# Ten input slots of a mixer: six ahead of the attention, four between its heads

## The reference

```python
x = layer_norm(ALPHA * x + 0.5 * swiglu(x, ffn1...))
proj = x @ w_in[l]                              # 1024 -> 2560
u, gb, gc, h, q, k, v = jnp.split(proj, splits, axis=-1)   # 256,256,256,256,512,512,512
y_a = pool_mixer(u, pool_w[l], pool_scale[l])   # window means 2,4,8,16 minus u, then a product by groups
y_b = gated_conv_mixer(gb, gc, h, conv_w[l])    # gb * conv3(gc * h)
y_c = neighbourhood_attention(q, k, v, rpb[l])  # 8 heads of 64, bias and mask, softmax
y = jnp.concatenate([y_a, y_b, y_c], axis=-1) @ w_out[l]
x = layer_norm(ALPHA * x + y)
x = layer_norm(ALPHA * x + 0.5 * swiglu(x, ffn2...))
```

## Time and profile before

| | us |
|---|---|
| median of 3 runs | 2865.69 |
| the profiled execution | 2866.16 |
| its span in the trace | 2864.3 |
| ten slots, layer 1: from the first piece to the end of the last | 216.89 to 275.67 |
| pooling's product and attention, layer 1 | 275.67 to 303.66, 27.99 |
| the same, layer 2 | 790.72 to 818.88, 28.16 |

### The profile page before, as it was taken

The page is one execution under the profiler, slowest core; times in us unless marked ns, Lnnn a source line. Parts: engine busy times, 40 slices in busy tenths (PEclk is TensorE's granted clock), DMA queues, the critical chain, the costliest instruction groups (busy, mean ns, idle before and its releaser), DMA issues.

```text
span 2864.3 us, 51977 instructions
## 1 busy us (share of the span) xinstructions
PE 2746.6 (96%) x21608; PEld 2534.5 (88%) x21608; DVE 1593.2 (56%) x2293; ACT 1299.3 (45%) x1847; POOL 439.1 (15%) x183
## 2 busy tenths in 40 slices
PE   8999999999999999999899899999999999989998
PEld 7988799899969989988899798999998789978898
DVE  5557655755766565556632815555555753452555
ACT  4444544444454444456524455444445543445443
POOL 0000000000000000014125670000003313764000
PEclk9999999999999999999999999999999999999999
DMA  8765366576536646663314454665673332454563
GB/s 233 214 184 169 92 188 184 170 217 192 161 94 187 186 145 194 185 171 108 94 53 126 152 180 125 185 188 160 186 214 111 96 90 61 162 159 135 160 185 124
DMA packets 622972, 445.42 MB, mean 156 GB/s; under 512 B 28048, under 2 KB 589488, under 8 KB 622320
## 3 DMA queue, kind: packets, MB, share of 16 engines
q1 hardware_dynamic: 622832, 443.43, 52.3%
HBM read 442.32 MB, written 1.05 MB: 155 GB/s over the span
## 4 chain that ended last, share of the span: by engine, by line
PE 77%; DVE 9%; POOL 6%; issue 5%; ACT 3%; DMA 0%; SPq 0%; DVEq 0%; POOLq 0%; ACTq 0%
PE ps L388 17%; PE ps L390 16%; PE ps L389 16%; PE ps L404 6%; PE ps L405 6%; PE ps L406 6%; POOL w_lo L889 6%; PE ps L670 1%; PE ps L646 1%; DVE w_lo L889 1%; PE ps L1595 1%; PE ps L1585 1%; ACT w_hi L685 1%; DVE sq L947 1%; PE ps L1557 1%
## 5 line engine op out<-in xcount | busy, mean ns | idle before, releaser
L388 PE MATMUL ps<-in_hi,w_hi 128*128 128x256 f32 x4352 | 1250.1, 287 | 27.4 <-DVE in_lo L963 7.6
L685 ACT ACTIVATE w_hi<-raw 128x1024 fp32r<-128x1024 f32 x800 | 845.6, 1057 | 921.2 <-PE ps L390 603.6
L390 PE MATMUL ps<-in_hi,w_lo 128*128 128x256 f32 x4352 | 1236.1, 284 | 0.0
L389 PE MATMUL ps<-in_lo,w_hi 128*128 128x256 f32 x4352 | 1235.9, 284 | 0.0
L889 DVE TENSOR_TENSOR w_lo<-raw,w_hi 128x1024 fp32r<-128x1024 f32 x622 | 760.6, 1225 | 696.6 <-ACT w_hi L685 695.5
L388 PEld LDWEIGHTS ps<-in_hi,w_hi 128*128 128x128 f32 x4352 | 839.0, 193 | 50.5 <-issue 13.7
L389 PEld LDWEIGHTS ps<-in_lo,w_hi 128*128 128x128 f32 x4352 | 839.2, 193 | 7.2 <-issue 0.5
L390 PEld LDWEIGHTS ps<-in_hi,w_lo 128*128 128x128 f32 x4352 | 838.8, 193 | 0.0
L889 POOL TENSOR_TENSOR w_lo<-raw,w_hi 128x1024 fp32r<-128x1024 f32 x178 | 438.5, 2470 | 2179.5 <-ACT w_hi L685 2178.6
L404 PE MATMUL ps<-w_hi,hid_hi 128*128 128x512 f32 x704 | 276.4, 393 | 1.2 <-DVE ps L1058 1.2
L405 PE MATMUL ps<-w_lo,hid_hi 128*128 128x512 f32 x704 | 276.0, 392 | 0.0
(11 more groups left out here) (327 smaller groups left out, 2636.5 us busy)
## 6 DMA issues: line engine op xcount, KB each, us to landing
raw<-in_w_ffn_in SPq DMA_DIRECT2D x176, 512.0 KB, 3.7
raw<-in_w_mix SPq DMA_DIRECT2D x112, 512.0 KB, 3.7
raw<-in_ffn_w_gate SPq DMA_DIRECT2D x88, 512.0 KB, 3.8
raw<-in_ffn_w_up SPq DMA_DIRECT2D x88, 512.0 KB, 3.7
raw<-in_ffn_w_down SPq DMA_DIRECT2D x88, 512.0 KB, 3.6
raw<-in_w_ffn_out SPq DMA_DIRECT2D x88, 512.0 KB, 3.6
raw<-in_w_in SPq DMA_DIRECT2D x40, 512.0 KB, 3.7
raw<-in_w_out SPq DMA_DIRECT2D x32, 512.0 KB, 4.2
```

The costliest lines, as they stand in the source:

```text
L388: nc.tensor.matmul(o, lh, rh, start=first, stop=False, **kw)
L389: nc.tensor.matmul(o, lh, rl, start=False, stop=False, **kw)
L390: return nc.tensor.matmul(o, ll, rh, start=False, stop=last, **kw)
L685: nc.scalar.activation(w_hi[:, e % SPLIT, :], raw[:, e % RAW, :], ACT.Copy).then_inc(sem("split_high"), 1)
```

## The change: what it does

The slots are loaded and multiplied in the order q, q, k, k, v, v, pool, gate c, h, gate b (`SLOTS1_ORDER`). The first six are multiplied ahead of the attention, as before. The eight pieces of the other four are multiplied by `fill` in the iterations i = 0 to 7 of TensorE's attention loop, one in each, and the pooling's product in i = 8. ScalarE's splits for them, and the copies of the four slots, go into `take`, at the end of its iterations. VectorE's low parts for the pieces three further on go into `beside(i)`, i = 0 to 7, at the end of its iterations; behind them there stand the pooling's sums (i = 2) and means (i = 3), the convolution's first two steps (i = 6), its other taps (i = 7) and its last product (i = 8). The bias masks move ahead, between the low parts of the six slots. The splits of the mixers' result move to i = 8 and later.

```diff
+SLOTS1, HEAD_SLOTS = 10, 6
+SLOTS1_ORDER = (4, 5, 6, 7, 8, 9, 0, 2, 3, 1)
...
 # TensorE
-                pe_linear(pe, 0, E1_IN, [features] * 8 + [tokens] * 2, C1_IN, TOGETHER)
+                pe_linear(pe, 0, E1_IN, [features] * 4 + [tokens] * 2, C1_IN, TOGETHER)
...
+                def fill(pieces):
+
+                    i = next(filled)
+                    if i < 2 * (SLOTS1 - HEAD_SLOTS):
+                        q, c = HEAD_SLOTS + i // 2, i % 2
+                        e = E1_IN + 2 * HEAD_SLOTS + i
+                        if c == 0 and q >= HEAD_SLOTS + 2:
+
+                            pe.wait_ge(sem("linear_taken"), q - 1)
+                        pe.wait_ge(sem("split_low"), e + 1)
+                        for _, o, left, right, first, last in features(2 + q % 2, e - c)[c]:
+                            mm = three(o, left, right, first, last, skip_group_check=True)
+                        mm.then_inc(sem("piece_used"), 1)
+                    elif i == 2 * (SLOTS1 - HEAD_SLOTS):
...
-                pe_attention(pe, "att", NA_HEADS, scores, values)
+                pe_attention(pe, "att", NA_HEADS, scores, values, fill)
...
 # ScalarE
+                def take(pieces):
+
+                    i = next(taken)
+                    if i < 2 * len(others):
+                        act_split(act, E1_IN + 2 * HEAD_SLOTS + i + SPLIT)
+                        if i % 2:
+                            nc.scalar.activation(others[i // 2], two_tiles(2 + (HEAD_SLOTS + i // 2) % 2), ACT.Copy)\
+                                .then_inc(sem("linear_taken"), 1)
+                    elif i == 2 * len(others):
+                        act.wait_ge(sem("pool_ready"), 1)
...
-                act_attention(act, "att", NA_HEADS, outs, beside=beside)
-                act_in_split(act, C1_OUT, mix1, mixed, first=2)
+                act_attention(act, "att", NA_HEADS, outs, take, beside)
+                act_in_split(act, C1_OUT, mix1, mixed, first=3)
...
 # VectorE
                 def beside(i):
-                    if i == 1:
-                        low_part(dve, E1_OUT + 2)
-                    if i in (3, 4):
-                        dve_in_split(dve, C1_OUT, mix1, first=i - 3, end=i - 2)
-
-                dve_double_bias(dve, steps, 1)
+                    if i < NA_HEADS:
+                        low_part(dve, E1_IN + 2 * HEAD_SLOTS + 3 + i)
+                    if i == 2:
+                        pool_sums()
+                    if i == 3:
+                        pool_means()
+                    if i == 6:
+                        dve.wait_ge(sem("linear_taken"), HEAD_SLOTS + 3)
+                        steps.link(nc.vector.tensor_tensor(conv_z[:, :, 1:S + 1], gate_c[:, :, :], conv_h[:, :, :], ALU.mult))
+                        conv_taps(1)
+                    if i == 7:
+                        conv_taps(0, 2)
+                    if i == 8:
+                        dve.wait_ge(sem("linear_taken"), SLOTS1)
...
                 dve_attention(dve, steps, "att", NA_HEADS, 64 ** -0.5,
                               lambda h, t: na_bias[:, h, (2 - 2 * t) * GRID:(6 - 2 * t) * GRID], beside)
-                dve_in_split(dve, C1_OUT, mix1, first=2)
+                dve_in_split(dve, C1_OUT, mix1)
...
 # SyncE
-                sp_linear(sp, E1_IN, columns(w_in[l], 10, (8, 9)))
+                sp_linear(sp, E1_IN, columns(w_in[l], SLOTS1, (8, 9), SLOTS1_ORDER))
```

More of the change, by code:

```diff
@@ L11 @@
+import itertools
 from contextlib import ExitStack
@@ L1784, in _ @@
                 pe_ln_turn(pe, 1)
-                pe_linear(pe, 0, E1_IN, [features] * 8 + [tokens] * 2, C1_IN, TOGETHER)
+                pe_linear(pe, 0, E1_IN, [features] * 4 + [tokens] * 2, C1_IN, TOGETHER)
                 pe.wait_ge(const_here, 32)
[L1789 to L1794, removed]
+                filled = itertools.count()
+                def fill(pieces):
[10 more added lines that the diff above has]
+                    elif i == 2 * (SLOTS1 - HEAD_SLOTS):
+                        pe.wait_ge(sem("linear_taken"), SLOTS1 - 1)
+                        pe.wait_ge(sem("pooled"), 1)
+                        pe.wait_ge(sem("pool_w_here"), 64)
+                        for c in range(2):
+                            mm = nc.tensor.matmul(ps[:, 2, c * S:(c + 1) * S], pool_w[:, c, :], pooled[:, c, :],
+                                                  start=True, stop=True)
+                        mm.then_inc(sem("pool_ready"), 1)
                 def scores(h, t):
                     o = 64 * (h % 2)
-                    pe.wait_ge(sem("linear_taken"), min(9 + h, 10))
+                    pe.wait_ge(sem("linear_taken"), min(HEAD_SLOTS - 1 + h, HEAD_SLOTS))
                     return [(na_q[o:o + 64, h // 2, t * P:(t + 1) * P], na_k[o:o + 64, h // 2, :])]
@@ L1891, in _ @@
                 act.wait_ge(sem("pool_pads"), 1)
-                dests = [pool_in[:, :, POOL_PAD:POOL_PAD + S], gate_b[:, :, :], gate_c[:, :, :], conv_h[:, :, :],
-                         na_q[:, 0:2, :], na_q[:, 2:4, :], na_k[:, 0:2, :], na_k[:, 2:4, :],
-                         na_v[:, :, 0:S], na_v[:, :, S:2 * S]]
+                dests = [na_q[:, 0:2, :], na_q[:, 2:4, :], na_k[:, 0:2, :], na_k[:, 2:4, :], na_v[:, :, 0:S], na_v[:, :, S:2 * S]]
                 act_linear(act, 0, E1_IN, dests)
[L1896 to L1900, removed]
+                others = [pool_in[:, :, POOL_PAD:POOL_PAD + S], gate_c[:, :, :], conv_h[:, :, :], gate_b[:, :, :]]
+                taken = itertools.count()
+                def take(pieces):
[7 more added lines that the diff above has]
+                        act.wait_ge(sem("pool_ready"), 1)
+                        for c in range(2):
+                            nc.scalar.activation(mix1[:, c, :], ps[:, 2, c * S:(c + 1) * S], ACT.Copy,
+                                                 scale=vec1[:, V1["pool_scale"] + c:V1["pool_scale"] + c + 1])\
+                                .then_inc(sem("pool_out"), 1)
                 def outs(h):
@@ L2091, in _ @@
[L2091 to L2115, removed]
@@ new lines, in _, with pool_sums @@
+                dve_double_bias(dve, steps, 1)
+                lows(E1_IN + 10, E1_IN + 2 * HEAD_SLOTS + 3)
+                def pool_sums():
+                    n = S + 2 * POOL_PAD
+                    dve.wait_ge(sem("linear_taken"), HEAD_SLOTS + 1)
+                    steps.link(nc.vector.tensor_tensor(sum2[:, :, 0:n - 1], pool_in[:, :, 0:n - 1], pool_in[:, :, 1:n], ALU.add))
+                    steps.link(nc.vector.tensor_tensor(sum4[:, :, 0:n - 3], sum2[:, :, 0:n - 3], sum2[:, :, 2:n - 1], ALU.add))
+                    steps.link(nc.vector.tensor_tensor(sum8[:, :, 0:n - 7], sum4[:, 1:2, 0:n - 7], sum4[:, 1:2, 4:n - 3], ALU.add))
+                    steps.link(nc.vector.tensor_tensor(sum16[:, :, 0:n - 15], sum8[:, :, 0:n - 15], sum8[:, :, 8:n - 7], ALU.add))
@@ new lines, in pool_means @@
+                def pool_means():
+                    cnt = cst("pool_cnt", 2 * S).rearrange("p (c t) -> p c t", c=2)
+                    for g, (w, sums) in enumerate(zip(POOL_W, (sum2[:, 0], sum4[:, 0], sum8[:, 0], sum16[:, 0]))):
+                        o = 64 * (g % 2)
+                        lo = POOL_PAD - w // 2
+                        ins = nc.vector.tensor_tensor(pooled[o:o + 64, g // 2, :], sums[o:o + 64, lo:lo + S],
+                                                      cnt[o:o + 64, g // 2, :], ALU.mult)
+                    steps.link(ins)
+                    nc.vector.tensor_tensor(pooled[:, :, :], pooled[:, :, :], pool_in[:, :, POOL_PAD:POOL_PAD + S],
+                                            ALU.subtract).then_inc(sem("pooled"), 1)
@@ new lines, in conv_taps @@
+                def conv_taps(*taps):
+                    for tap in taps:
+                        for c in range(2):
+                            w = vec1[:, V1["conv_w"] + 2 * tap + c:V1["conv_w"] + 2 * tap + c + 1]
+                            z = conv_z[:, c, tap:tap + S]
+                            if tap == 1:
+                                ins = nc.vector.tensor_scalar(conv_y[:, c, :], z, w, None, ALU.mult)
+                            else:
+                                ins = nc.vector.scalar_tensor_tensor(conv_y[:, c, :], z, w, conv_y[:, c, :], ALU.mult, ALU.add)
+                        steps.link(ins)
@@ L2271, in d_rows, with columns @@
                 return d[:, c // P:c // P + 1, :] if isinstance(c, int) else d[:, bass.ds(c // P, 1), :]
-            def columns(w, n, token_slots=()):
-                for i in range(n):
+            def columns(w, n, token_slots=(), order=None):
+                for i in order or range(n):
                     c = i * S
```

19 lines of the change are left out of this document (6 added, 13 removed).

## The result

The changed kernel took 2876.5 us (median of 7, 2871.09 to 2880.8), the kernel before 2868.61 us in the same comparison (median of 7). The ratio is 1.0025, 95% interval 1.0013 to 1.0036: slower by 3.7 to 10.3 us. In a second comparison of the same pair it was 1.0031 (1.0019 to 1.0044). 2881 us was forecast, 2868 to 2889 as the range. The medians are 7.9 us apart, where the forecast's sum had 15.7.

What follows compares the result with a forecast made beforehand. TensorE, busy 96%, was taken to bound the kernel, but a ScalarE-VectorE loop to pace the changed attention: 2866.16 + 11.5 (loop) + 4.2 (clock) = 2881.9 us profiled, median 0.5 lower, stated as 2881; range 2868 to 2889.

Steps and rivals of the forecast that it cites:

- The loop: Attention: ScalarE's split, VectorE's low part, next bias, maximum and exponentials form a 5.60 us turn, against TensorE's 5.54 per iteration.
- walk: Step-by-step sum along the loop from T to the output product: 56.87 us, against 51.03 before.
- T: End of the sixth slot (the twelfth piece), where the walk starts; 252.63 in the kernel before.
- additions: VectorE's pooling sums, means and convolution steps behind the low part, 6.17 us inside the loop, plus taps, 1.82.
- The clock: Half clock after the stalls of heads 6 and 7: 2.1 us per layer, 4.2 in all.
- such a fall would cost nothing: Clock loss after an earlier attention stall, as head 6's, lies in the next stall; only that after head 7's counts.
- The stalls: TensorE idles about 2 us ahead of head 3's transposes and about 4 us each ahead of heads 6 and 7.
- The sum: Whole kernel: 2866.16 + 11.5 + 4.2 = 2881.9 us for the profiled execution.
- A: Rival: busy sums decide, all TensorE idling in the two attentions goes, -5.8 and -5.9 us, 2854; chance 0.08.
- B: Rival: loop holds but pooling and convolution find gaps, 48.9 us per layer, -2.2 each, 2861; chance 0.07.
- C: Rival: head 3's stall also loses clock and the first split shows, another 2.5 + 1.3 us per layer, 2889; chance 0.11.
- the first split: Split of the mixers' result, expected to end before TensorE's product needs it; otherwise about 0.6 + 0.7 us per layer.

Runs made afterwards that it cites:

- the warm matmuls: Changed kernel plus 3, 7 and 7 idle TensorE matmuls ahead of its waits for the probabilities of heads 3, 6 and 7; ratio 1.0016 to the kernel before.
- the kernel with the loop opened: Changed kernel with each VectorE low part one iteration later, behind the next head's maximum; ratio 0.9948 to the kernel before.
- the kernel with the additions moved: Changed kernel with pooling and convolution ahead of the low part in VectorE's `beside(i)`; ratio 0.9983 to the kernel before.
- the changed kernel again: Changed kernel run and profiled a second time, no edit; ratio 1.0031 to the kernel before.

## Why the prediction was right

- **The loop.** The prediction's walk gave 54.52 us from T to the last transposes; the profiles show 54.51 and 54.47. Its terms held one by one, as the splits above show. That the additions are inside it is shown by two experiments, one taking them out (7.2 us less; 8.0 by the walk, and nearly all of the rest is the 0.6 us by which the sums and means outlast the waits into which they were put) and one adding to them (2.9 us more, 2.9 expected). That the loop closes through the low part ahead of the next bias is shown by the one that opens it there, which ends at 46.8 us.
- **The clock.** I took 2.1 us per layer, 4.2 in all, within 0 to 2.5. Against the warm matmuls it cost 1.25 us in each layer of the first profile, 2.5 in all, and 2.0 and 2.5 in the second, 4.5 in all. So the term was 1.7 us too large for the execution that it was meant for and about right for the next one; which of the two a run gets was not foreseen, and that 2.1 met the second is luck as much as reading. The mechanism was right, for the loss counts behind the last stall. Expecting it of the stalls of about 4 us alone was not: the stall of 1.74 us at head 3 was followed by half clock in one profile (0.50 from 282.7 to 289.5) and by full clock in the other. That such a fall would cost nothing was right: nothing later moved.
- **The stalls.** Forecast were about 2, 4 and 4 us, some 10 per attention. Measured were 1.74, 1.26 and 3.95 in one profile, 7.0 in all, and 1.74, 3.98 and 3.08 in the other, 8.8. The half clock makes the difference: where TensorE works more slowly ahead of a wait, the wait is shorter.
- **The sum.** +15.7 us was forecast for the profiled execution, and it was +13.0 (2879.17 against 2866.16). At the output product of layer 2 it stood at 832.32 - 818.88 = 13.4; the two stages gave 58.12 - 51.03 and 58.11 - 51.20, 14.0 together, less some 0.6 gained ahead of them. As timed the change costs much less, 7.9 us by the medians and 7.2 by the ratio. Of the 13.0 us about 5 are the luck of the two executions that were profiled: the one before lies 2.5 us under the median of its seven runs, the one after 2.7 us over its own. The direction and the place of the loss were forecast rightly, its size as timed twice too large.
- **The rivals.** A, the busy sums, is refuted for this kernel, with a remark: its time is near that of the kernel with the loop opened, 46.8 us a layer against the 45.3 of A. The Trainium skill's advice to interleave regimes (Perfetto Trace Analysis, Optimization Strategy) holds in this case's runs once the order allows it (ratios 0.9983 and 0.9948 for the same work in other places of the lists), and not before (1.0025). B, additions that find gaps, describes the kernel with the additions moved (50.5 us per layer, 48.9 by B's sum), not the changed one. C did not happen: the stall of head 3 did lower the clock in the first profile, but the loss vanished in the later waits, and the first split did not show.
- **What stays open.** As timed the change costs 3.7 to 12.6 us by the two intervals, its two stages 14 and 15.4 in the two pairs of profiles (from T past the output product). All kernels built on the change come out 4 to 7 us better than their stages, by the ratios; the kernel against itself does not (1.0004). Behind the output product of layer 2, in parts that no kernel here changes, the profiles took from 2040.0 to 2046.7 us, and both of the kernel before lie high, at 2045.4 and 2045.6. One lead is the clock: over a whole run it was granted at 0.981 in the mean of 46 timed runs of the kernel before, and at 0.9815 to 0.986 in the means of the kernels built on the change, and among those 46 the longest runs have the low clock (2875 to 2877 us at 0.976 to 0.979, 2858 us at 0.982 and 0.983). Whether that is luck or a link to the changed part was not tested.

## What to carry to other kernels

When two engines hand work to each other inside one iteration, add up one turn start to start, with every instruction that stands between a wait and the next hand-over, and compare that sum with the bound engine's iteration, before believing busy shares. If the turn is as long as the iteration, there is no free place in it: put other work ahead of the wait, where the engine idles anyway, or take the waiting instruction one iteration later, so that it finds its input there. A stall that is removed can come back one instruction further down another engine's list, so read that list too. And measure a stage up to a point well behind it: what a stall costs through the clock can fall into the next one.

## What the runs showed of the hardware that was not expected

The granted clock does not fall at the same places from one execution to the next, with the same instructions in the same order. Besides 282 to 291 above, a stretch in the second layer of the second block shows it. Both kernels do the same work here, 120 us behind the first transposes of a norm. Before:

```profile
2274.70:2284.70 10.00, 4.32 (x30) 4.11 (x30) 9.47 (x22) 1.75 (x2) 0.00 (x0) 0.82 0.03 8
2284.70:2294.70 10.00, 10.00 (x52) 7.96 (x50) 2.69 (x6) 5.88 (x9) 0.00 (x0) 0.84 0.33 98
```

And the changed kernel again, the same work:

```profile
2291.90:2301.90 10.00, 4.31 (x25) 4.11 (x24) 7.86 (x20) 1.06 (x1) 0.00 (x0) 0.66 0.19 55
2301.90:2311.90 10.00, 10.00 (x63) 7.96 (x62) 4.73 (x7) 8.28 (x12) 0.00 (x0) 1.00 0.20 56
```

The half level takes about the same time in both, 3.6 + 3.2 and 6.8 us of these 20 (from the mean clocks 0.82, 0.84 and 0.66), but in the kernel before 3.2 us of it lie over dense work. From the first transposes of that norm to the first matmul of L1549 (L1552 in the changed kernel) it took 193.2 to 193.4 us in seven of nine profiles and 189.6 and 189.7 in two. A difference of 3.7 us between single profiles is therefore nothing that a change of a few microseconds could be read from; the stage that was changed has to be read by itself.
